# Second layer's expert rows added up in four open PSUM banks instead of scattered and read back; first modulation loads issued ahead of the barrier

## The chip, the cores and the metric

The kernel runs on one core of a Trainium2 chip, as one launch. The metric is the device time of that core in microseconds. The core has a matrix engine (TensorE, PE in the profile, with its weight loads as PEld), a vector engine (DVE), a scalar engine (ACT), GpSimd (POOL) and a sync engine (SP, whose DMA issues stand as SPq), and 16 DMA engines that all of them share. Each engine runs its own instruction stream; the streams meet at semaphores. Matmul results go to PSUM, here eight banks of 128 x 512 float32.

## The reference, cut to what matters

Two layers over 256 context tokens and 256 latent tokens of width 1024, float32. Each layer has a token-mixing half (projection, attention and recurrent heads, output projection) and a channel-mixing half, a mixture of 64 experts with 8 chosen per token. Every half is modulated by vectors that come from `silu(c) @ w_ada`. The second layer returns the latent tokens only.

```python
mod_l = (silu_c @ w_ada[l] + b_ada[l]).reshape(b, 6, 1, D_MODEL)...   # and mod_c from silu(c_ctx)
x_c, x_l = token_mixing(...)
...
# channel mixing; h is (tokens, 1024), 512 tokens in layer 0, 256 in layer 1
scores = sigmoid(h @ router_w); idx = top 8 of the allowed experts; w = scores[idx] / sum * 2.5
def run_block(tok, wt, e):
    xb = h[tok]
    hid = silu(xb @ w_gate[e]) * (xb @ w_up[e])          # 1024 -> 256
    return (hid @ w_down[e]) * wt[:, None]               # 256 -> 1024
y = segment_sum(rows of all experts, token) + shared expert
x_l = x_l + gate_l * rms_norm(y, g_post)
```

## The kernel before

All of it is one Bass program with hand-written semaphores; `build` loops over the two layers (`l`, with `last` for the second), and each engine has one block of code per layer. A first block ahead of an all-engine barrier loads the tokens `X`, the constants and the two condition vectors `HC` (lines 436 to 441), and ACT and DVE prepare small things from them.

**Start of a layer.** SP loads a static list of weight pieces into a ring of three slots: four pieces of `w_ada` (2 MB each, line 508), five of `w_in` (lines 510 to 514), and later ones. Piece n waits until PE has finished with piece n-3. PE first turns the normalised tokens (`transposes`, line 968), then multiplies the four modulation pieces (`ada_piece`, line 978), DVE modulates (line 1433), and the projections follow (lines 1012 and 1015).

**Experts.** The pairs of token and expert are packed into units of 32 rows of one expert; two units (`un` 0 and 1) are a block of 64 slots. Layer 0 runs some 80 blocks, layer 1 runs 48. A row of 1024 is kept as two half rows of 512 on two partitions, so a block fills 128 partitions. SP streams the experts' weights, 3 MB each, through four slots (`load_up` line 533, `load_down` line 538); the gate and up part of a slot is free after the block that used it last has done its up product, the down part after the down product (`reload`, lines 548 and 551). For each block:

- DVE picks the block's table columns and makes a one-hot matrix `OH` (`one_hot`, lines 1749 to 1753); PE multiplies it with token numbers and ranks (`meta`, line 1237, into bank 7); DVE turns the result into a gather index `GIX` and a scatter index `SIXT` (`rows`, lines 1760 to 1765).
- POOL gathers 128 half rows from DRAM `hrows` (line 680) into one of two buffers `XG`. PE turns them (line 1244), ACT moves them to `XGT` (line 913), PE does the gate and up product in 16 matmuls of 32 columns each, four side by side (`up`, line 1254), of which the last four come after the turn of the hidden rows of the block before (line 1313). A float32 matmul is counted as two in the profile, so a block's `up` is x24 and x8.
- ACT and DVE form the hidden rows (lines 919, 923, 1777, 1779). PE does the down product into bank 2 (`down`, line 1279), ACT copies it to one of two `YSB` (line 941), and POOL scatters the 128 half rows to DRAM `yrows` (line 699), at a place for each token and each of its 8 choices. ACT waits on the scatter of two blocks ago before it writes the same `YSB`.

PE's loop is pipelined: iteration b does `up` of block b+1, then the turn of tokens of block b+2, then `down` of block b, then `meta`.

**End of a layer.** When the last scatter has landed, SP reads `yrows` back (line 589, eight loads of 1 MB in layer 1), half of the choices of a token is weighted and added by DVE (line 1820), half by PE with diagonal matrices `DG` (line 1387) that ACT makes from the weights `WK` (DVE, line 1713, one instruction for each tile and choice). DVE adds both to the shared expert's rows in `YS`, then comes the norm (ACT line 952 and 954, DVE lines 1806 to 1811) and the store (line 593).

## Time and profile before

| | us |
|---|---|
| median of 3 runs | 2045.66 |
| lowest, highest | 2041.65, 2048.55 |
| profiled execution, its own time | 2038.08 |
| its span | 2036.3 |
| busy: PE, DVE, ACT, POOL | 1608.0, 898.2, 574.4, 347.3 |
| mean DMA rate | 284 GB/s |

The span is that of one profiled execution. 1.8 us lie around it. The timeline gives, for each group of instructions, its start, its length, the engine, the line, output and input and their shapes, the count, and in brackets how long the engine was idle ahead of it and what ended that. The table of windows gives busy time by engine, the granted clock of PE (1.00 is 2.4 GHz, 0.50 is 1.2 GHz), and the DMA engines' busy share and rate. The stages of the span: layer 0 up to about 1134 us, of which the experts take from about 510 to 1077; layer 1's token mixing to about 1408; layer 1's routing to about 1457; its experts to 1998; its end to 2036.3.

### The profile page before, as it was taken

Reading aid. Unit: us, or ns where it says so; the run is one execution under the profiler, and the core shown is the slowest. Engines: PE = TensorE matmul, PEld = TensorE weight load, DVE = VectorE, ACT = ScalarE, POOL = GpSimd, SP = SyncE. Lnnn points to the kernel's source line nnn. Section 1 sums busy time; section 2 is a strip of 40 time slices with the busy share of each in tenths; the row PEclk is TensorE's granted clock in tenths of the full one; section 3 lists DMA queues with packets and bytes.
Section 4 is the critical chain, followed back from the end, with each engine's and each line's share of the span. In section 5 each row is a group of like instructions: output and inputs, shape, how many; then the busy total and the mean of one; then the engine's idle time right before and its main releaser. Section 6 shows DMA issues by size and latency. Waiting matters only on the chain. (4 is left out here: it accounts for less than half of the span.)

```text
span 2036.3 us, 39515 instructions
## 1 busy us (share of the span) xinstructions
PE 1608.0 (79%) x11503; PEld 697.9 (34%) x11504; DVE 898.2 (44%) x3018; ACT 574.4 (28%) x1197; POOL 347.3 (17%) x357
## 2 busy tenths in 40 slices
PE   3999689868989899888896499867767666766685
PEld 2544554422333333323332365544322222221221
DVE  2154683444444444444455426553533332322334
ACT  2142372222332333323332215143112221211222
POOL 0002300012222222222220001030121111211220
PEclk8999899999999999999998789978888887878998
DMA  8313710467999989998847743624699999999974
GB/s 280 135 70 134 281 64 1 186 234 289 388 405 413 391 348 406 413 358 346 342 156 309 245 152 124 250 105 155 238 410 403 413 401 413 412 405 380 409 308 188
DMA packets 165603, 578.28 MB, mean 284 GB/s; under 512 B 24956, under 2 KB 29792, under 8 KB 148648
## 3 DMA queue, kind: packets, MB, share of 16 engines
q1 hardware_dynamic: 134592, 515.49, 64.7%
q0 software_dynamic: 24256, 60.03, 7.9%
q10 hardware_dynamic: 6696, 1.98, 0.4%
q8 instruction: 37, 0.61, 0.1%
q14 instruction: 22, 0.18, 0.0%
HBM read 557.87 MB, written 37.89 MB: 293 GB/s over the span
## 5 line engine op out<-in xcount | busy, mean ns | idle before, releaser
L1254 PE MATMUL bank<-arena 128*32 128x512 f32 x4160 | 539.1, 638 | 167.4 <-DMA arena<-in_exp_w_up 139.6
L1279 PE MATMUL bank<-arena 128*32 128x512 f32 x2048 | 249.3, 600 | 68.2 <-issue 67.7
L699 POOL DMA_INDIRECT yrows<-arena x128 | 130.1, 1016 | 858.3 <-ACT arena L941 858.3
L1254 PEld LDWEIGHTS bank<-arena 128*32 128x32 f32 x4160 | 125.4, 114 | 355.6 <-issue 327.3
L935 ACT ACTIVATE arena<-bank 128x128 f32<-128x128 f32 x128 | 35.6, 278 | 629.5 <-PE bank L1313 629.5
L1777 DVE TENSOR_TENSOR arena<-arena,bank 64x512 f32<-64x512 f32 x130 | 88.4, 680 | 258.6 <-ACT arena L919 258.6
L680 POOL DMA_INDIRECT arena<-hrows,arena x134 | 137.2, 1024 | 132.5 <-DVE arena L1765 91.9
L1749 DVE COPY arena<-arena 128x12 bf16 (+1 forms) x272 | 60.5, 223 | 188.9 <-issue 188.9
L1012 PE MATMUL bank<-arena 128*128 128x512 f32 (+3 forms) x384 | 132.4, 507 | 11.7 <-DVE arena L1433 11.7
L941 ACT ACTIVATE arena<-bank 128x512 f32<-128x512 f32 x128 | 76.5, 597 | 166.8 <-PE bank L1279 166.8
L1279 PEld LDWEIGHTS bank<-arena 128*32 128x32 f32 x2048 | 60.3, 109 | 163.4 <-issue 161.7
L1244 PEld LDWEIGHTS bank<-arena 128*128 128x128 f32 x528 | 74.0, 209 | 113.3 <-issue 110.8
L1244 PE MATMUL bank<-arena 128*128 128x128 f32 x528 | 98.9, 310 | 2.6 <-issue 1.5
L1012 PEld LDWEIGHTS bank<-arena 128*128 128x128 f32 x384 | 78.0, 214 | 64.4 <-issue 45.8
L1015 PE MATMUL bank<-arena 128*128 128x512 f32 (+1 forms) x256 | 100.0, 552 | 0.0
L919 ACT ACTIVATE arena<-bank 64x512 f32<-64x512 f32 x130 | 77.3, 594 | 40.0 <-PE bank L1254 37.2
L1760 DVE COPY arena<-bank 128x3 f32<-128x3 f32 x134 | 21.8, 163 | 150.2 <-PE bank L1237 149.0
L1175 PE MATMUL bank<-arena 128*128 128x512 f32 x192 | 82.9, 593 | 1.1 <-DVE arena L1613 1.1
L1779 DVE TENSOR_TENSOR arena<-arena 64x256 f32<-64x256 f32 x130 | 54.5, 419 | 65.2 <-ACT arena L923 65.2
L1753 DVE TENSOR_TENSOR arena<-arena 128x512 bf16<-128x512 f32 (+1 forms) x136 | 80.2, 590 | 4.7
L913 ACT ACTIVATE arena<-bank 128x512 f32<-128x512 f32 x132 | 78.8, 597 | 8.0 <-PE bank L1244 3.1
L1313 PEld LDWEIGHTS bank<-arena 64*128 64x128 f32 x256 | 39.6, 201 | 115.9 <-issue 115.9
(305 smaller groups left out, 1856.7 us busy)
## 6 DMA issues: line engine op xcount, KB each, us to landing
arena<-in_exp_w_gate SPq DMA_DIRECT2D x128, 1024.0 KB
arena<-in_exp_w_up SPq DMA_DIRECT2D x128, 1024.0 KB
arena<-in_exp_w_down SPq DMA_DIRECT2D x128, 1024.0 KB
arena<-in_w_ada SPq DMA_DIRECT2D x10, 3072.0 KB, 12.0
arena<-yrows SPq DMA_DIRECT2D x24, 1024.0 KB, 16.3
arena<-in_w_ada SPq DMA_DIRECT2D x8, 2048.0 KB, 12.7
arena<-in_w_in SPq DMA_DIRECT2D x8, 2048.0 KB, 13.4
arena<-in_w_out SPq DMA_DIRECT2D x4, 2048.0 KB, 9.9
```

The source lines that it names most:

```text
L680: pool.indirect_dma_start(out=XG[k], out_offset=None, in_=hrows, in_offset=bass.IndirectOffsetOnAxis(ap=GIX[k], axis=0), bounds_check=2 * ...
L699: pool.indirect_dma_start(out=yrows, out_offset=bass.IndirectOffsetOnAxis(ap=SIXS[u], axis=0), in_=YSB[u], in_offset=None, bounds_check=2 ...
L913: act.activation(XGT, bank[4][:, :].rearrange("p (c u h s) -> p c u h s", c=4, u=2, h=2), ACT.Copy).then_inc(a_xe, 1)
L919: act.activation(HL[0:64, :], bank[0][64:128, :], ACT.Copy).then_inc(a_lo, 1)
L1012: ins = pe.matmul(bank[o % 4][:, c0:width], HT[:, c, tile_of(j)], w[:, c, c0:], start=(c == 0), stop=(c == 7))
L1015: ins = pe.matmul(bank[o % 4][:, c0:], w[:, c, tile_of(j)], HT[:, c, c0:], start=(c == 0), stop=(c == 7))
L1175: ins = pe.matmul(bank[2 * t + hf][:, :], MT[:, c, tile_of(t)], w[:, c, :], start=(c == 0), stop=(c == 7))
L1244: ins = pe.transpose(bank[4][:, c * P:(c + 1) * P], XG[par][:, c:512:4], IDENT)
L1254: ins = pe.matmul(bank[0][r:r + UNIT, :], XGT[:, c, un, hh, :], wv[un][:, :, hh, c, :], start=(c == 0), stop=(c == 3))
L1279: ins = pe.matmul(bank[2][r:r + UNIT, :], HIDT[:, c, UNIT * un:UNIT * un + UNIT], wv[un][:, c, cg * 512:(cg + 1) * 512], start=(c == 0), s ...
L1753: dve.tensor_tensor(OH[:, T0:], IOTA.rearrange("p (u n) -> p u n", u=2).unsqueeze(1).broadcast_to([P, NTS, 2, SLOTS]), RR[:, T0:].unsqueez ...
L1777: dve.tensor_tensor(HL[0:64, :], HL[0:64, :], bank[0][0:64, :], ALU.add).then_inc(v_gu, 1)
```

## The change

**First loads.** Three loads of `w_ada` for layer 0 (6 MB) are issued ahead of the barrier, behind `X` and the constants; the two loads of the condition vectors move to the front. The semaphores of these early loads are new (`sp_first`), so that the ones the ring counts on are not cleared by the barrier. PE does modulation piece 0 ahead of the transposes of the tokens.

**Layout in both layers.** In a block, the half h of a row now lies on partitions 64h to 64h+63 (it was interleaved with the units), so `OH` is half as wide and `meta` writes both halves from the same one-hot. DVE then takes each unit's columns by a mask in two instructions (`picked`), where one copied them.

**Layer 1.** No scatter, no `yrows`, no read-back, no `WK` and no `DG`. The shared expert's down product goes to banks 6, 7, 3 and 1 and stays open there: (6, 7) are the two column halves of token tile 2, (3, 1) of tile 3. `meta` also sums up the slot's weight, split in three bfloat16 parts (`KVW`), and moves to bank 5; PE waits for `v_mc` (DVE has read them) ahead of the third quarter of `up`. DVE keeps token and weight of each slot in `SLOTW` and builds for each block `OHW`, 128 partitions by 2 tiles by 128 tokens: the weight where slot and token meet, else zero. In iteration b PE adds block b-1: four float32 matmuls of 64 rows by 128 columns over 512 (`combine`), just ahead of `down`. There is one `YSB`; ACT writes it when `combine` has read it. POOL no longer scatters, and clears `XG` (128 x 512) ahead of each gather. At the end PE adds the last block, and norm, residual and store work on the banks by halves of 512 columns.

```diff
             def _(sp):
+                sp.dma_start(HC[:, 0, :], ...).then_inc(sp_first[0], 16)
+                sp.dma_start(HC[:, 1, :], ...).then_inc(sp_first[0], 16)
                 for t in range(2):
-                    sp.dma_start(X[:, t, :], ...).then_inc(sp_land[0], 16)
+                    sp.dma_start(X[:, t, :], ...).then_inc(sp_first[2], 16)
...
+                for n in range(3):
+                    sp.dma_start(at(ring[n], 8, 512), w_ada[:, :, n * 512:(n + 1) * 512]).then_inc(sp_land[n], 16)
+                sp.wait_ge(sp_first[2], 64)
-        nc.all_engine_barrier(sems_to_clear=all_sems)
+        nc.all_engine_barrier(sems_to_clear=sems_behind_first)
...
+                if l == 0:
+                    ada_piece(0, 0, 512)
                 transposes(0, (0, 1, 2, 3))
-                for n in range(N_ADA1):
+                for n in range(1 if l == 0 else 0, N_ADA1):
...
                 def shared_down(j):
-                    if j >= 2:
+                    if j >= 2 and not last:
                         pe.wait_ge(a_sd, j - 1)
                     for k in range(2):
-                        ins = pe.matmul(bank[2 + hf][:, :], ..., start=(k == 0), stop=(k == 1))
+                        ins = pe.matmul(bank[acc[j // 2][hf] if last else 2 + hf][:, :], ...,
+                                        start=(k == 0), stop=(k == 1 and not last))
...
+                def combine():
+                    for i in range(2):
+                        for cg in range(2):
+                            r = slice(SLOTS * cg, SLOTS * cg + SLOTS)
+                            ins = pe.matmul(bank[acc[i][cg]][:, :], OHW[r, i, :], YSB[0][r, :], start=False, stop=False)
+                    return ins
...
                         pe.wait_ge(v_hid, b + 1)
+                        if last:
+                            pe.wait_ge(v_mc, b + 4)
                         up(ks, range(2, 3), False)
...
+                    if last:
+                        pe.wait_ge(a_y, b + 2)
+                        pe.wait_ge(v_ow, b + 1)
+                        combine().then_inc(pe_cmb, 1)
                     pe.wait_ge(a_h, b + 1)
                     pe.wait_ge(a_y, b + 2)
...
             # POOL, in the loop
                         pool.sem_inc(pool_go, 1)
+                        if last:
+                            pool.memset(XG[(u + 1) % 2], 0.0).then_inc(pool_z, 1)
+                            pool.wait_ge(pool_z, i * 2 + (u + 2))
                         gather((u + 1) % 2)
+                        if not last: (v_six, a_y, scatter to yrows as before)
...
             # DVE
+                def picked(n, chain):
+                    chain(dve.tensor_scalar(MA[:, 0:NKV], META[:, 0:NKV], COLS[:, 7:8], None, ALU.mult))
+                    dve.scalar_tensor_tensor(out=M3[:, 0:NKV], in0=META[:, NKV:2 * NKV], scalar=COLS[:, 8:9], in1=MA[:, 0:NKV],
+                                             op0=ALU.mult, op1=ALU.add).then_inc(v_mc, 1)
+                def weighted(b, chain):
+                    chain(dve.tensor_copy(S2, SLOTW[:, :, bass.ds(b, 1)].rearrange("p a n -> p (a n)")))
+                    dve.wait_ge(pe_cmb, b + 1)
+                    dve.tensor_scalar(OHW.rearrange(...), IOTA2.rearrange(...), S2[:, 0:1], S2[:, 1:2],
+                                      ALU.is_equal, ALU.mult).then_inc(v_ow, 1)
...
             # DVE, end of layer 1
+                    for i, t in enumerate(TS):
+                        dve.tensor_tensor(SSO[:, t:t + 1], S8[...], S8[...], ALU.add).then_inc(v_so, 1)
+                        dve.wait_ge(a_fs, i + 1)
+                        link(dve.reciprocal(RSTD[:, t:t + 1], SSTD[:, t:t + 1]))
+                        for hf in range(2):
+                            link(dve.scalar_tensor_tensor(out=YS[:, t, c], in0=bank[acc[i][hf]][:, :], ...))
+                            dve.tensor_tensor(X[:, t, c], X[:, t, c], YS[:, t, c], ALU.add).then_inc(v_end, 1)
```

How the change stands in the instruction streams. First PE's loop of layer 1, between the turn of the tokens of block b+2 and the first down product; ISA and TENSOR_LOAD rows are register work. Before:

```order
L1244 MATMUL bank<-arena 128x128 [waits pool_g1]
L1244 MATMUL bank<-arena 128x128 x3
L1361 UNCONDITIONAL_BRANCH
L1363 ISA
L1285 TENSOR_LOAD arena
L1285 ISA x2
L1300 ISA [waits a_y,a_h]
```

And in the changed kernel (its line numbers), up to the branches that choose the weight slot:

```order
L1295 MATMUL bank<-arena 128x128 [waits pool_g1]
L1295 MATMUL bank<-arena 128x128 x3
L1421 UNCONDITIONAL_BRANCH
L1423 ISA
L1336 TENSOR_LOAD arena
L1336 ISA x2
L1366 MATMUL bank<-arena 128x512 [waits v_ow,a_y]
L1366 MATMUL bank<-arena 128x512 x3
L1351 ISA [waits a_y,a_h]
```

Four matmuls come in between the register work and the branches, in every block.

Second, SP at the start of the program, before:

```order
L436 DMA arena<-in_ctx 128x1024
L437 DMA arena<-in_x 128x1024
L438 DMA arena<-in_consts 128x656
L439 DMA arena<-in_consts 128x384
L440 DMA arena<-in_c_ctx 128x8
L441 DMA arena<-in_c 128x8
L432 UNCONDITIONAL_BRANCH [waits sp_land0]
L497 UNCONDITIONAL_BRANCH [waits barrier_Pool_Activation_PE_DVE_SP_release]
L508 DMA arena<-in_w_ada 128x8x512 x3
```

and after, where the three large loads stand ahead of the wait and of the barrier:

```order
L455 DMA arena<-in_consts 128x656
L456 DMA arena<-in_consts 128x384
L459 DMA arena<-in_w_ada 128x8x512 x3
L447 UNCONDITIONAL_BRANCH [waits sp_first2]
L513 UNCONDITIONAL_BRANCH [waits barrier_Pool_Activation_PE_DVE_SP_release]
```

## Rows read from the trace of the kernel before

**Rows 1.** The page's part 2: DMA busy share in 40 slices of 50.9 us.
```profile
DMA  8313710467999989998847743624699999999974
```

**Rows 2.** DMA queues, 1500 to 1950: GB/s in 40 slices; packets, MB, share.
```profile
GB/s 412 414 412 415 412 401 379 412 411 414 412 414 398 407 375 416 412 414 415 411 413 412 413 408 414 412 390 403 413 412 412 375 399 316 391 416 414 411 413 357
...
q1 hardware_dynamic: 36733, 167.75, 92.5%
q0 software_dynamic: 6240, 13.94, 8.0%
```

**Rows 3.** Waits, 1460 to 2000: who for whom, us in total, times, longest.
```profile
PE bank L1254 <- DMA arena<-in_exp_w_up: 137.0, 24, 10.8
...
PE bank L1279 <- issue: 18.4, 28, 1.4
```

**Rows 4.** Windows: length, busy us of PE, PEld, DVE, ACT, POOL, clock, DMA share, GB/s.
```profile
1460.00:1972.00 512.00, 348.10 (x2634) 117.37 (x2626) 162.06 (x677) 114.11 (x228) 90.76 (x89) 0.86 1.00 401
...
1344.70:1346.90 2.20, 2.14 (x6) 0.63 (x6) 0.00 (x0) 1.29 (x2) 2.20 (x5) 0.50 0.06 8
```

**Rows 5.** Timeline of PE: a block after a DMA wait, and one without.
```profile
1558.44 4.58 PE L1254 MATMUL bank<-arena 128*32 128x512 f32 x24 [9.76 <-DMA arena<-in_exp_w_up]
...
1981.15 2.78 PE L1254 MATMUL bank<-arena 128*32 128x512 f32 x24 [0.33 <-issue]
...
1986.79 1.92 PE L1279 MATMUL bank<-arena 128*32 128x512 f32 x16 [0.81 <-issue]
...
1989.18 2.78 PE L1254 MATMUL bank<-arena 128*32 128x512 f32 x24 [0.31 <-issue]
```

**Rows 6.** Timeline of PE: attention scores, two float32 matmuls of 64 rows each.
```profile
1344.76 2.08 PE L1122 MATMUL bank<-arena 64*128 64x512 f32 x4 [0.69 <-ACT arena L859]
...
1357.66 1.13 PE L1122 MATMUL bank<-arena 64*128 64x512 f32 x4
```

**Rows 7.** Timeline of POOL: two memsets of 128 x 512.
```profile
1412.80 1.02 POOL L668 MEMSET arena<- 128x512 f32 x2
```

**Rows 8.** Timeline of DVE in layer 1's routing: first and last of the weights.
```profile
1435.33 0.22 DVE L1713 SCALAR_TENSOR_TENSOR arena<-arena 128x64 f32<-128x64 f32 x1
...
1439.60 0.42 DVE L1699 TENSOR_TENSOR arena<-arena,bank 128x256 f32<-128x256 f32 x1
```

**Rows 9.** Timeline of all engines from the last down product to the end.
```profile
1996.75 0.60 ACT L941 ACTIVATE arena<-bank 128x512 f32<-128x512 f32 x1 [1.54 <-PE bank L1279]
...
1998.21 1.02 POOL L699 DMA_INDIRECT yrows<-arena  x1 [5.53 <-ACT arena L941]
...
2019.21 1.28 ACT L954 ACT_TABLE_LOAD   x1
...
2024.28 1.98 PE L1387 MATMUL bank<-arena 128*128 128x512 f32 x4 [0.52 <-DMA arena<-yrows]
...
2030.72 1.22 DVE L1811 TENSOR_TENSOR arena<-arena 128x1024 f32<-128x1024 f32 x1
```

**Rows 10.** Timeline at token mixing's end: square, scale and add on 512 columns.
```profile
1407.68 0.60 ACT L890 ACTIVATE arena<-bank 128x512 f32<-128x512 f32 x1 [6.18 <-PE bank L1175]
...
1409.12 0.75 DVE L1645 SCALAR_TENSOR_TENSOR arena<-bank,arena 128x512 f32<-128x512 f32 x1
...
1411.29 0.69 DVE L1647 TENSOR_TENSOR arena<-arena 128x512 f32<-128x512 f32 x1
```

**Rows 11.** Timeline of the first 52 us, SP and PE.
```profile
12.17 15.96 SPq L508 DMA_DIRECT2D arena<-in_w_ada  x4
...
19.13 6.55 PE L968 MATMUL bank<-arena 128*128 128x128 f32 x32 [19.13 <-DVE arena L1404]
...
39.67 3.58 PE L978 MATMUL bank<-arena 128*2 128x128 f32 x64 [3.12 <-DMA arena<-in_w_ada]
...
51.09 1.25 PE L1012 MATMUL bank<-arena 128*128 128x264 f32 x2 [5.86 <-DVE arena L1433]
```

**Rows 12.** DMA rate, 0 to 60 us, in 40 slices of 1.5 us.
```profile
GB/s 0 224 366 410 412 333 14 0 0 187 395 382 360 342 351 393 385 397 388 380 374 378 346 359 339 326 308 254 124 244 170 180 195 218 273 368 403 401 351 165
```

More of the change, by code:

```diff
@@ L274, in build @@
         sp_land = [sem(f"sp_land{k}") for k in range(3)]
+        sp_first = [sem(f"sp_first{k}") for k in range(3)]
         sp_up = [sem(f"sp_up{k}") for k in range(NSLOT)]
@@ L404, in build @@
         a_dg = sem("a_dg")
-        v_ys = sem("v_ys")
-        v_fs = sem("v_fs")
+        v_mc = sem("v_mc")
+        v_ow = sem("v_ow")
+        pe_cmb = sem("pe_cmb")
+        pool_z = sem("pool_z")
         v_end = sem("v_end")
@@ L675, in _ @@
                 pool.wait_ge(pool_hr, 16 * NTS)
[L676 to L677 removed]
+                if last:
+                    pool.memset(YSB[0], 0.0).then_inc(pool_clr, 1)
+                    pool.memset(OHW, 0.0).then_inc(pool_clr, 1)
+                else:
+                    for k in range(2):
+                        pool.dma_start(hrows[k:k + 1, :], X[0:1, 0, 0:512]).then_inc(pool_s[k], 16)
                 def gather(k):
@@ L905, in _ @@
                     act.activation(SHS[:, K0:], bank[2 + 2 * k][:, K0:], ACT.Silu).then_inc(a_sh, 1)
-                for j in range(2 * NTS):
+                for j in range(0 if last else 2 * NTS):
                     act.wait_ge(pe_sd, j + 1)
@@ L1661, in _ @@
                 dve.wait_ge(v_pcl, 6)
-                link(dve.tensor_scalar(KV[:, :, :, 0], KV[:, :, :, 0], COLS[:, 0:1], None, ALU.add))
-                for t in range(NT):
-                    link(dve.memset(KV[:, t, :, 1], float(P * t)))
+                link(dve.tensor_scalar(KVX[:, :, :, 0], KVX[:, :, :, 0], COLS[:, 0:1], None, ALU.add))
+                for i in range(2 if last else NT):
+                    link(dve.memset(KVX[:, i, :, 1], float(P * (i + T0 if last else i))))
+                if last:
+                    for i in range(2):
+                        link(dve.tensor_scalar(IOTA2[:, i, :], IOTA, float(P * (T0 + i) + 1), None, ALU.add))
                 dve.wait_ge(pe_rtt, 1)
@@ L1704, in _ @@
                 link(ins)
-                link(dve.tensor_scalar(KV[:, T0:, :, 2], ci, -1.0, float(T), ALU.add, ALU.mult))
+                if not last:
+                    link(dve.tensor_scalar(KV[:, T0:, :, 2], ci, -1.0, float(T), ALU.add, ALU.mult))
                 wsum = WSUM[:, T0:]
@@ L1782, in _ @@
                 pairs = dve.value_load(NPR[0:1, 0:1], min_val=1, max_val=MAXB // 2 + 1)
-                PER = 7
+                PER = 9 if last else 7
+                if last:
+                    dve.wait_ge(pool_clr, 11)
+                    dve.sem_inc(v_ow, 1)
                 with dve.Fori(0, pairs) as i:
```

311 lines of the change are left out of this document (193 added, 118 removed).

## The prediction, made before the changed kernel was run

> **What bounds the kernel now.** I read the slices of the page first: DMA is at 9 tenths or more through the last third and drops only in the last two slices, the end of the kernel [rows 1]. So layer 1's experts live on the weight stream, and what follows them does not. The queue view says how close: from 1500 to 1950 most slices stand at 411 to 416 GB/s, fourteen or so are lower; against 414 they lose some 10 us. Of the traffic 13.94 MB are indirect transfers, which took 8.0% of the 450 us, and weights took 92.5% [rows 2]. The waits confirm it from the other side: PE stood 137.0 us for weights, in 24 waits, the longest 10.8, and 18.4 us for nothing but its own sequencer ahead of the down products [rows 3]. The window 1460 to 1972 is 512 us for 48 blocks at a DMA share of 1.00 [rows 4], 10.7 us each; without PE's waits, 512 - 154 (137 and 17 more that the weight loads waited) = 358 us, or 7.5 us of work each. Two clocks are mixed in that: a block after a long wait starts with x24 in 4.58 us, one without a wait in 2.78, and such a block lasts 1989.18 - 1981.15 = 8.0 us [rows 5].
>
> **Scatter traffic.** Gather and scatter move the same rows, so half of the indirect share goes: 4% of 450 us is 18 us, for 38 of 48 blocks; with the other blocks up to 1972 some 19.5 us. This is the gain of the stream if it stays full.
>
> **combine.** PE gets four float32 matmuls of 64 rows over 512 columns in every block, not in the trace of before. The nearest row is the score product, two such matmuls on opposite row halves and into different banks, as here: 1.13 us at full clock, 2.08 where the window reads a clock of 0.50 [rows 4, 6]. Two matmuls of 128 rows take 1.98 at full clock (L1387 at 2024.28 in [rows 9]), so the halves do run side by side. Four cost 2.0 to 2.3 us at 2.4 GHz. They are issued ahead of the branches that choose the slot, and today PE idles 0.2 to 1.1 us there (0.81 in the block shown [rows 5]); I let 0.6 of that be covered. Net 1.4 us a block. Bounds: 0.9, if all of the gap is covered; 3.5, if the pairs run at 1.2 GHz (2 x 2.08 less 0.6). I take the full clock, because every block shown ends its up product at the full rate even where it began slow. 48 x 1.4 = 67 us of new work against PE's 154 us of slack: PE does not become the bound on average.
>
> **What that does to the stream.** The down part of a slot is given back after `combine`, and in a run of blocks without a wait each block gives its slots back 1.4 us later than now. A wait of PE for weights that lasts 9 or 10 us swallows the lateness; a queue that runs dry inside a run does not. The slices below 411 GB/s show that it runs dry a dozen times already [rows 2], with some two blocks to a run (48 blocks, 24 waits [rows 3]). Lower bound of the new loss: nothing. Upper: 12 x 2 x 1.4 = 34 us. I take the middle, 17 us: stage 19.5 - 17 = 2.5 us shorter. I am least sure of this term. At the end, after the last weights have landed, three blocks run at PE's pace (starts at 1973.97, 1981.15 and 1989.18): + 3 x 1.4 = 4 us.
>
> The Trainium skill (TensorEngine Tiling, Key Properties) speaks against the change: changing the tiling mode drains TensorE, and `combine` puts one more mode between the token turn and the down product. It gives no price. The row pair bounds it: 1.13 us against 1.0 for four quarter-size steps at the steady rate, 0.13 a drain. By the rule, with two drains a block, the term is 1.7 us in place of 1.4 and the total 4 us worse. The sum does not use it.
>
> **DVE, ACT and POOL in a block.** DVE gains one masking step, two small steps for the weight, the copy to `S2` and `OHW` (256 columns), about 1.2 us in all, and loses half of `OH` and the scatter index. Its streams end 6.4 us after `meta` of an 8.0 us block, so it stays inside 9.4. PE's new waits: `v_mc` comes from DVE's second step behind `meta`, while PE has 1.9 us of up product first; `v_ow` comes behind the hidden rows, which PE waits for anyway. Behind a late one stand `combine`, `down` and the slot's release. POOL's clearing is 0.51 us [rows 7] ahead of a gather that no longer stands behind a scatter, and has two blocks of time. All nothing. Layer 0 gets the masking step and the half `OH`: nothing either, since PE sets the pace there at 7.7 us a block and DVE's one-hot is ready 2.4 us ahead of its matmul.
>
> **Routing of layer 1.** The 16 weight instructions go, 1435.33 to 1439.60 [rows 8], but the next step waits for the shared expert's product, which PE ends at 1438.64. So 0.9 us come, and the three added links of the first index chains take them back. Nothing.
>
> **The end.** Now: the last copy ends at 1997.35, the last scatter is issued at 1998.21, then come landing, read-back and sums up to 2026.3, norm and residual up to 2031.94, and the store to 2036.3 [rows 9]. After: copy, one pair of the last `combine` (1.1), two squares on 512 columns (0.6 and 0.2 each: 1.65), add and semaphore 0.4, table load 1.28, root 0.3, reciprocal 0.4, two halves of scale and add 2.86 (1409.12 to 1411.98 [rows 10]); then tile 3, whose root waits for DVE's add behind tile 2: 0.9 and 2.86; then the store, 4.36 as now. The sum with hops is 16.8 us behind 1996.7, against 39.6. Gain 22.8 us.
>
> **The front.** The first `w_ada` load is issued at 12.17 [rows 11]; the DMA engines are idle from 9.0 to 13.5 us, then busy to 46 [rows 12]. With the loads queued behind the constants this gap closes: 4.5 us, less 0.9 for two small issues now ahead of `X`. On top, piece 0 is multiplied before the transposes (19.13 to 25.6), so piece 3 is issued some 11 us earlier and no longer shares the stream with `w_in`; it ends the wait at 39.67 that leads through DVE to the projections at 51.09 [rows 11]. Between 3.6 and 6.6, I take 5 us. From 51.09 PE is busy without a break, so it stays.
>
> **Sum** against the profiled execution: - 5 - 2.5 + 4 - 22.8 = - 26.3 us, 2036.3 to 2010. The median of the runs is 2045.66, 7.6 above the profiled execution's 2038.08; set off from it, 2019.
>
> **Rivals.**
> 1. The stream stays full, as PE's slack of 154 us would have it: then the 17 us don't arise, 2002. For it: waits of 9 us and more swallow six added blocks. Against it: the dry slices.
> 2. PE binds over long stretches: three-block runs become longer than the weights of three experts (3.15 MB at 0.41 MB a us is 7.7 us, a block 9.4), the 34 us arise and the stage is 14.5 us longer than now: 2045.66 - 5 + 14.5 + 4 - 22.8 = 2036.
> 3. Slower than before: `combine` runs at 1.2 GHz, 3.5 us net [rows 6]. Per block 7.5 + 3.5 = 11 us; 48 are 528, and with the 16 us of dry slices now 544 in place of 512: + 32, the last three blocks + 10.5, less 27.8 = + 15, 2060. It decides from about 3.1 us a block. Against it: the half clock shows after waits only [rows 5], and `combine` stands 6 us into a block.
> 4. The early loads don't do what they should: they share the engines with `X` and the constants, the barrier comes later, the front gives nothing. 2024, within the range.
>
> **How the numbers follow.** Forecast 0.50 (2010 to 2027), rival 1 0.22, rival 2 0.16, rival 3 0.04, rival 4 0.08. The range takes in rival 1 and most of rival 2: 2001 to 2035. A measurement here tells 0.3%, 6 us, from no change: same is 2039.5 to 2051.8, to which a strong rival 2 reaches. Faster 0.92, same 0.04, slower 0.04.
>
> **What would show it.** The combine row: x8 in 2.0 to 2.3 us, and a gap ahead of the down product under 0.5. The weight window 3 us or so shorter, with a lower DMA rate than 401 GB/s. PE's wait for weights down from 137 to 60 or 80 us. From the last down product to the end 17 us. The first L1012 (now at 51.09) at 46. Wrong would be: combine groups over 3 us, or a stage whose DMA rate stays at 401 and whose length drops by all 19 us, or waits of PE on `v_ow` or `v_mc`.

## The result, and the profile after

The changed kernel took 1976.65 us (median of 4 runs, 1975.49 to 1985.36), the kernel before beside it 2043.66 (4 runs, 2041.44 to 2048.55): a ratio of 0.968, with a 95% interval of 0.964 to 0.971. That is 67 us less; forecast were 2019 us and a range of 2001 to 2035. The time lies 24 us below the range. Set against each other, the two profiled executions differ by 61.5 us (spans 2036.3 and 1974.8), and they can be cut at four points that both traces show:

| stretch | before, us | after, us | difference | forecast |
|---|---|---|---|---|
| start to the first up product of layer 0 | 436.9 | 429.0 | - 7.9 | - 5 |
| layer 0's experts, to the start of the last down product | 637.6 | 618.1 | - 19.5 | 0 |
| from there to the first up product of layer 1 | 382.5 | 381.8 | - 0.7 | 0 |
| layer 1's experts, to the start of the last down product | 537.8 | 528.3 | - 9.5 | + 1.5 |
| from there to the end | 41.5 | 17.6 | - 23.9 | - 22.8 |

The end and, roughly, the front came as forecast. Two stretches did not: layer 1's experts lost 9.5 us instead of gaining 1.5, and layer 0's experts, of which nothing was expected, lost 19.5. In the changed file L1305 is the up product (L1254 before), L1330 the down product (L1279), L1371 the turning of the hidden rows (L1313), L969 ACT's copy of them (L935), L1366 `combine`.

**Layer 1's experts.** First the window from the first up product to the end of the weight stream, of the changed kernel (columns as in [rows 4]):

```profile
1429.00:1931.00 502.00, 423.72 (x3002) 144.95 (x3003) 191.02 (x822) 113.93 (x228) 70.36 (x92) 0.93 1.00 398
```

and the same window of the kernel before:

```profile
1457.00:1978.00 521.00, 355.47 (x2684) 119.63 (x2684) 166.03 (x697) 114.99 (x230) 93.80 (x92) 0.86 1.00 399
```

PE does 68 us more and the engines of the DMA are full in both (share 1.00, 398 and 399 GB/s). PE's granted clock rose with it, from 0.86 to 0.93. The stream is 19 us shorter at the same rate, which is what was forecast for the scatter's traffic. Of a queue that runs dry behind `combine` nothing is seen. Where PE's new work went is in the waits, 1428 to 1960 (who for whom, us in total, times, longest), against 137.0 us in 24 waits before [rows 3]:

```profile
PE bank L1305 <- DMA arena<-in_exp_w_up: 63.4, 15, 6.8
```

The other part of PE's new work stands behind the stream. The DMA rate in 40 slices of 1.5 us, from 1900 on after, and from 1940 on before:

```profile
GB/s 414 401 410 410 350 421 330 396 396 407 423 426 415 415 410 418 421 418 371 60 49 0 0 0 0 0 0 0 0 0 0 0 0 0 0 0 0 0 0 0
```

```profile
GB/s 418 401 426 399 360 221 178 322 374 223 355 414 421 440 426 393 423 401 429 418 412 372 257 259 60 27 0 0 0 109 0 0 0 0 79 3 0 0 0 0
```

After, the last weight packet starts at 1931.2 and the last down product at 1957.2, 26.0 us later; before, they start at 1978.2 and 1994.8, 16.6 us apart. PE's timeline of the changed kernel in that stretch:

```profile
1940.98 0.23 PE L1288 MATMUL bank<-arena 128*64 128x10 bf16 x4
1941.48 2.78 PE L1305 MATMUL bank<-arena 128*32 128x512 f32 x24 [0.26 <-issue]
1944.19 0.45 PE L1371 MATMUL bank<-arena 64*128 64x64 f32 x2
1944.57 1.06 PE L1305 MATMUL bank<-arena 128*32 128x512 f32 x8
1945.57 0.75 PE L1295 MATMUL bank<-arena 128*128 128x128 f32 x4
1946.24 1.99 PE L1366 MATMUL bank<-arena 64*128 64x512 f32 x8
1948.16 1.92 PE L1330 MATMUL bank<-arena 128*32 128x512 f32 x16
1950.02 0.23 PE L1288 MATMUL bank<-arena 128*64 128x10 bf16 x4
1950.53 2.78 PE L1305 MATMUL bank<-arena 128*32 128x512 f32 x24 [0.28 <-issue]
```

`combine` takes 1.99 us, and neither ahead of it nor behind it is there a gap: the down product starts at 1948.16, before the record of `combine` ends. A block lasts 9.05 us where two blocks before lasted 7.2 and 8.0 [rows 5]: + 1.4 on their mean, as forecast.

**The end.** The timeline of all engines from the last copy on, the rows that answer to [rows 9]:

```profile
1959.20 0.60 ACT L978 ACTIVATE arena<-bank 128x512 f32<-128x512 f32 x1 [2.69 <-PE bank L1330]
1960.09 1.99 PE L1450 MATMUL bank<-arena 64*128 64x512 f32 x8 [0.80 <-ACT arena L978]
1961.26 0.60 ACT L986 ACTIVATE arena<-bank 128x512 f32<-128x512 f32 x1 [1.46 <-PE bank L1450]
...
1962.68 1.28 ACT L989 ACT_TABLE_LOAD   x1
...
1970.18 0.69 DVE L1938 TENSOR_TENSOR arena<-arena 128x512 f32<-128x512 f32 x1
```

Landing, read-back and eight sums are gone; the chain is the one that was written down. From the last down product to the end it is 17.6 us against 41.5.

**The front.** SP's and PE's timeline of the first 44 us (before: [rows 11]):

```profile
4.88 7.74 SPq L459 DMA_DIRECT2D arena<-in_w_ada  x3
19.79 0.54 SPq L526 DMA_DIRECT2D arena<-in_w_ada  x1
```

```profile
16.14 3.59 PE L1026 MATMUL bank<-arena 128*2 128x128 f32 x64 [16.14 <-DMA arena<-in_w_ada]
...
28.02 3.55 PE L1026 MATMUL bank<-arena 128*2 128x128 f32 x121
33.49 2.15 PE L1026 MATMUL bank<-arena 128*2 128x128 f32 x71 [1.93 <-issue]
...
43.45 11.90 PE L1062 MATMUL bank<-arena 128*128 128x264 f32 x40 [5.86 <-DVE arena L1510]
```

Piece 3 is issued when the first product has given back slot 0, at 19.79, and no wait for a DMA stands ahead of its product any more, where before PE waited 3.12 us for it. The projections start at 43.45 in place of 51.09.

**Layer 0's experts.** Here the two traces differ in one row. The kernel before, PE and ACT from one turning of the hidden rows to the down product:

```profile
612.85 1.02 POOL L680 DMA_INDIRECT arena<-hrows,arena  x1 [0.31 <-issue]
...
613.13 0.45 PE L1313 MATMUL bank<-arena 64*128 64x64 f32 x2
...
614.41 0.28 ACT L935 ACTIVATE arena<-bank 128x128 f32<-128x128 f32 x1 [3.75 <-PE bank L1313]
```

```profile
616.18 1.88 PE L1279 MATMUL bank<-arena 128*32 128x512 f32 x13 [0.93 <-issue]
```

The transposes end at 613.58, but ACT's copy of their result starts 0.83 us later, and PE, which waits for the copy ahead of the down product and has its branches to take behind it, stands idle for 0.93. I call this the late copy: one that starts more than 0.1 us behind the transposes. It is there in 76 of the 80 blocks of layer 0, by 0.2 to 1.2 us, 0.92 at the median, and in 26 of the 48 of layer 1. In the changed kernel it is there in 33 of 80 in layer 0 and in none of layer 1; where it is missing, the copy starts 0.04 us behind the transposes:

```profile
601.45 1.02 POOL L705 DMA_INDIRECT arena<-hrows,arena  x1 [0.58 <-issue]
601.46 0.31 PEld L1371 LDWEIGHTS bank<-arena 64*128 64x128 f32 x2 [0.84 <-issue]
601.46 0.45 PE L1371 MATMUL bank<-arena 64*128 64x64 f32 x2
601.94 0.28 ACT L969 ACTIVATE arena<-bank 128x128 f32<-128x128 f32 x1 [2.95 <-PE bank L1371]
```

PE's waits ahead of the down product, over layer 0, in the kernel before (437 to 1076.4) and the changed one (429 to 1047):

```profile
PE bank L1279 <- issue: 49.3, 76, 1.8
```

```profile
PE bank L1330 <- issue: 28.9, 40, 1.8
```

### The profile page after: what moved, and what is told of

It reads as the page before. It is cut to its first block and busy times, and to the rows that moved or that the text cites. A ratio compares the mean times of both kernels' runs of the same rounds, so it can differ in the third digit from the quotient of the medians.

```text
span 1974.8 us, 40623 instructions
## 1 busy us (share of the span) xinstructions
PE 1671.9 (85%) x11863; PEld 721.0 (37%) x11864; DVE 911.4 (46%) x3217; ACT 569.5 (29%) x1189; POOL 322.7 (16%) x358
## 5 line engine op out<-in xcount | busy, mean ns | idle before, releaser
L1305 PE MATMUL bank<-arena 128*32 128x512 f32 x4160 | 529.4, 628 | 100.8 <-DMA arena<-in_exp_w_up 69.1
L1330 PE MATMUL bank<-arena 128*32 128x512 f32 x2048 | 249.2, 601 | 30.4 <-issue 29.7
L1305 PEld LDWEIGHTS bank<-arena 128*32 128x32 f32 x4160 | 123.2, 113 | 283.6 <-issue 265.8
L969 ACT ACTIVATE arena<-bank 128x128 f32<-128x128 f32 x128 | 35.5, 277 | 496.1 <-PE bank L1371 483.9
L732 POOL DMA_INDIRECT yrows<-arena x80 | 81.1, 1013 | 408.8 <-ACT arena L978 408.8
L1836 DVE COPY arena<-arena 128x12 bf16 (+1 forms) x272 | 54.4, 200 | 188.1 <-issue 188.1
L1330 PEld LDWEIGHTS bank<-arena 128*32 128x32 f32 x2048 | 57.1, 109 | 155.1 <-issue 151.8
L1847 DVE TENSOR_SCALAR arena<-bank,arena 128x3 f32<-128x3 f32 (+1 forms) x134 | 29.8, 222 | 155.5 <-PE bank L1288 154.4
L1366 PE MATMUL bank<-arena 64*128 64x512 f32 x384 | 95.4, 615 | 0.0
L724 POOL MEMSET arena<- 128x512 f32 x48 | 25.2, 525 | 408.7 <-DVE arena L1865 408.7
```

Source lines behind the costliest of these rows:

```text
L732: pool.indirect_dma_start(out=yrows, out_offset=bass.IndirectOffsetOnAxis(ap=SIXS[u], axis=0), in_=YSB[u], in_offset=None, bounds_check=2 ...
L1305: ins = pe.matmul(bank[0][r:r + UNIT, :], XGT[:, c, hh, un, :], wv[un][:, :, hh, c, :], start=(c == 0), stop=(c == 3))
L1330: ins = pe.matmul(bank[2][r:r + UNIT, :], HIDT[:, c, UNIT * un:UNIT * un + UNIT], wv[un][:, c, cg * 512:(cg + 1) * 512], start=(c == 0), s ...
L1366: ins = pe.matmul(bank[acc[i][cg]][:, :], OHW[r, i, :], YSB[0][r, :], start=False, stop=False)
```

## The experiments

They ran in five sets; the kernels of a set share a chip and the runs of the kernel before. Those runs were the first finding: the kernel before took 2022.3, 2020.7, 2041.8, 2021.9 and 2020.0 us in the five, while it had taken 2043.7 in the shown pair. Ratios are to the kernel before in the same set.

### What made layer 0 faster: first set (before 2022.3)

Nearly all late copies of the shown traces have the gather 1.32 us behind the scatter's start; in the blocks of the changed kernel where it stood at 1.58, the copy was on time. So theory A was that the late copy comes from this distance, and that the change had moved it by the longer index chain. Two kernels put one small POOL step ahead of the gather, `e1_before_pool_step` on the kernel before and `e2_after_pool_step` on layer 0 of the changed one:

```diff
+pool.memset(SPACE, 0.0).then_inc(pool_nm, 1)
+pool.wait_ge(pool_nm, i * 2 + (u + 1))
+pool.sem_inc(pool_go, 1)
 gather((u + 1) % 2)
```

> The kernel before with one small POOL clearing (256 columns, some 0.3 us) and its wait ahead of each gather of the block loops, both layers. Theory A (timing of the gather): in the blocks of layer 0 that don't wait for weights, ACT's copy of the hidden rows (L935 before) starts 0.8 to 1.2 us behind the end of the two transposes, and always about 1.55 us behind the start of the gather, when the gather is issued 0.3 us behind the scatter's end; with 0.6 us or more between them, as in every second block of the changed kernel, it starts 0.04 us behind. Then the copy starts at once in all blocks, the gap ahead of the down product goes, a block takes 7.0 to 7.3 us in place of 7.88, and layer 0 is 35 to 60 us shorter. Theory B (the narrower one-hot or the new row layout made layer 0 faster): nothing here changes, 2044 us, or up to 0.3 us more a block.

> The changed kernel with the same POOL clearing and wait ahead of each gather of layer 0 alone. Theory A: the late copy goes in the other half of layer 0's blocks too (it is there in 40 of 80), 25 to 40 us less than the changed kernel, about 1945 us; the down-to-down period of layer 0 falls from 7.63 to 7.1 or 7.2. Theory B: as the changed kernel, 1977 us, or a little more.

Two others lengthen DVE's chain on the kernel before by the same two steps, ahead of the indices or behind them:

```diff
+chain(dve.tensor_copy(TK[:, 3:4], TK[:, 1:2]))
+chain(dve.tensor_copy(TK[:, 3:4], TK[:, 1:2]))
```

> The kernel before with two more one-column DVE copies in a chain ahead of the two indices of a block, so that the gather's index comes 0.4 to 0.5 us later. Nothing else changes; POOL has no new instruction. Theory A: the gather now starts 0.6 to 0.7 us behind the scatter's end in place of 0.3, the copy of the hidden rows starts at once, layer 0 is 35 to 60 us shorter. Theory B, and the theory that DVE's chain sets the pace: no gain, or up to 0.5 us a block more, 40 us longer.

> The kernel before with the same two DVE copies, but behind the indices and ahead of the one-hot. Theory A: the gather is issued as before, 0.3 us behind the scatter, so the late copy stays and layer 0 takes what it took, within 3 us. The rival of theory A that any longer DVE chain does it (fewer collisions of DVE with PE or POOL): as the run with the later index.

Measured: 2026.7 (ratio 1.002, 1.001 to 1.003), 1978.5 (0.979), 2024.3 (1.001, 0.999 to 1.002) and 2023.4 (1.000, 0.999 to 1.002). None of the four has one late copy in layer 0, not even e4, whose gather stands at 1.32 us in 75 of 78 places. Theory A as I had it is gone: a gather at 1.32 us is not enough for a late copy. The totals of e1, e3 and e4 lie outside every reading that I had written down, because the kernel before was 21 us faster in this set without any step; e2 came out near the 1977 of theory B, which says nothing for B, since the late copies were missing without a step as well.

### Is it the program or the execution: second set (before 2020.7)

> The kernel before, unchanged, profiled once more. In the three runs above that were built on it the kernel before took 2022 us where it had taken 2044, and none of them shows the late copy of the hidden rows, not even the one whose gather is issued 0.3 us behind the scatter in 75 of 78 places; so theory A as stated (the distance of the gather) has fallen. Theory C: the late copy belongs to the execution (the chip that it ran on), not to the program. Then this run, where it takes about 2022 us, has the copy 0.04 us behind the transposes in all blocks, a layer 0 of 617 to 622 us in place of 637.6, and a layer 1 of 535 to 542. Theory D: it belongs to the program and two more DVE steps or a POOL step are enough to end it; then the late copy is there in 76 of 80 blocks, whatever the total.

> The changed kernel, unchanged, on the same chip as the kernel before. Theory C: layer 0 takes the same as in the kernel before on this chip, within 3 us, and the change is worth 45 to 49 us here in place of 67 (7.6 at the front, 24 at the end, the rest in layer 1's experts). Theory D: 60 us or more, 20 of them in layer 0.

The kernel before, unchanged: 2023.0 us, no late copy, 613.7 us for layer 0 where the shown execution took 637.6. Its rows at the same place, the gather 1.32 us behind the scatter as ever:

```profile
611.23 1.01 POOL L699 DMA_INDIRECT yrows<-arena  x1 [8.33 <-ACT arena L941]
612.55 1.02 POOL L680 DMA_INDIRECT arena<-hrows,arena  x1 [0.31 <-issue]
...
612.84 0.45 PE L1313 MATMUL bank<-arena 64*128 64x64 f32 x2
613.33 0.28 ACT L935 ACTIVATE arena<-bank 128x128 f32<-128x128 f32 x1 [2.96 <-PE bank L1313]
```

and its waits ahead of the down product, over layer 0:

```profile
PE bank L1279 <- issue: 14.2, 30, 1.8
```

The changed kernel: 1976.2 us (ratio 0.978, 0.975 to 0.980), no late copy, 620.3 us for layer 0. So theory C holds in this: whether there are late copies at all comes with the execution and not with the program. The change is worth 44.5 us where it is absent (I had written 45 to 49) and 67 where it is present. Layer 0 then does not get shorter: 613.7 to 622.1 us over eight executions of the kernel before and its variants, 615.2 to 620.3 over six of the changed one and its variants. Beside c1, c2 is 6.6 us longer there, more than the 3 that I had allowed and inside this scatter. With late copies four executions of the changed kernel and its variants took 618.1 to 624.9 us. Its waits give a part of them back: without late copies PE waits 14.1 us for weights in layer 0, with 33 of them 5.6.

### The front (same set, and third set)

`e5_after_front_undone` issues the three loads behind the barrier and multiplies piece 0 behind the transposes; `e10_first_product_late` (third set, before 2041.8) puts back the product alone:

```diff
-if l == 0:
-    ada_piece(0, 0, 512)
 transposes(0, (0, 1, 2, 3))
-for n in range(1 if l == 0 else 0, N_ADA1):
+for n in range(N_ADA1):
```

> The changed kernel with the first three modulation loads issued behind the barrier and the first modulation product behind the transposes, as before. Prediction: 5 us longer than the changed kernel (3.6 to 6.6); by the changed kernel's trace, in which the first projection came 7.6 us earlier, 7 to 8 us. Rival: the early loads are worth nothing by themselves and the 7.6 us come from the order of the first inputs, which stays: under 2 us. Layer 0 and layer 1 take as long as in the changed kernel, within 2 us.

> The changed kernel with its early loads, but with the first modulation product behind the transposes, as before. With loads and product both put back the kernel took 7.4 us more. Prediction: the gap of 3.6 us belongs to the loads, the rest to the product ahead of the transposes, which lets piece 3 be issued earlier: so 1.5 to 4 us more than the changed kernel. Rival: everything comes from the loads, which are issued 7.3 us earlier (4.88 in place of 12.17): under 1 us.

Measured: e5 1983.6 against 1976.2, 7.4 us more; the projections start at 52.06, in c2 at 44.45. e10: 1987.8 us, and they start at 52.19, while two other variants of the changed kernel in its set (e7 and e9, below) have them at 45.23. Both readings of e10 missed, since it gives up 7.0 us where I had 1.5 to 4, or under 1: early loads without the early product give nothing at all. Its rows, of SP and PE:

```profile
4.58 8.16 SPq L459 DMA_DIRECT2D arena<-in_w_ada  x3
30.59 0.54 SPq L526 DMA_DIRECT2D arena<-in_w_ada  x1
```

```profile
28.60 5.42 PE L1026 MATMUL bank<-arena 128*2 128x128 f32 x192
40.78 3.60 PE L1026 MATMUL bank<-arena 128*2 128x128 f32 x64 [6.76 <-DMA arena<-in_w_ada]
```

Three pieces lie ready in three slots, but the fourth needs the first slot, and that comes free with the first product. It is issued at 30.59, and PE waits 6.76 us for it. In the kernel before it was issued at 27.59, in the changed one at 19.79: these 7.8 us are about the gain at the projections. What the early product gives without the early loads was not run.

### What combine costs (second and third set)

`e6_combine_8_columns` cuts `combine` in the loop to 8 of 512 columns, which leaves most of the routed sum out; `e7_combine_twice` issues it twice, which adds the routed rows twice. The edit of e6:

```diff
-ins = pe.matmul(bank[acc[i][cg]][:, :], OHW[r, i, :], YSB[0][r, :], start=False, stop=False)
+ins = pe.matmul(bank[acc[i][cg]][:, 0:8], OHW[r, i, :], YSB[0][r, 0:8], start=False, stop=False)
```

> The changed kernel with each of combine's four matmuls in a block cut to 8 of its 512 columns, which leaves most of the routed sum out of the output. What combine costs the stream. Prediction (the slots come back 1.4 us later and the queue runs dry behind them, 17 us in all, + 4 us in the last three blocks): layer 1's experts end 15 to 21 us earlier than in the changed kernel. Rival (the stream stays full, PE's waits swallow combine, as the trace with a DMA rate of 401 GB/s suggests): 3 to 6 us earlier, the last three blocks alone, while PE's waits for weights grow by 70 to 90 us.

> The changed kernel with combine's four matmuls issued twice in each block of the loop, so that the routed rows are added twice. With combine once, the weight transfers of layer 1's experts take 501 to 503 us from first to last and the last down product starts 26 us behind their end; with 8 columns of it 503.6 and 16.5. Theory E (PE's waits for weights, 63 us, are the only buffer; as long as some are left the stream does not feel PE): 48 x 2.0 = 96 us of new work against 63 us of waits, so the buffer is used up; layer 1's experts get 30 to 40 us longer and the waits go to under 10 us. The prediction's dry queue (each added microsecond per block costs the stream a third of itself at once): 17 us for 1.4 a block gives 24 us more for 2.0, and the waits are not used up (30 us or more are left).

| kernel | combine, us a block | first up product to end of weights | PE's waits for weights | granted clock | end of weights to last down product |
|---|---|---|---|---|---|
| e6, 8 columns | 0.6 | 501.4 | 111.4 | 0.87 | 16.5 |
| c2, changed kernel | 2.0 | 500.4 | 62.7 | 0.94 | 25.6 |
| shown, changed kernel | 2.0 | 502.3 | 63.4 | 0.93 | 26.0 |
| e7, twice | 3.9 | 503.1 | 12.4 | 0.98 | 36.7 |

e6 does not take `combine` away, but cuts it to a third; its row is

```profile
1936.95 0.62 PE L1366 MATMUL bank<-arena 64*128 64x8 f32 x8
```

e6 took 1966.7 us against 1976.2, e7 1996.7 in a set with late copies, in which the changed kernel was not run. The 9.5 us of e6 lie between my two readings, 15 to 21 and 3 to 6, and its waits grew by 49 us in place of 70 to 90. The waits of PE in e7, from 1435 to 1976:

```profile
PE bank L1305 <- issue: 14.6, 22, 7.7
PE bank L1305 <- DMA arena<-in_exp_w_up: 12.4, 6, 3.4
```

`combine` costs the stream nothing, not even twice: its length stays within 3 us. The waits pay the larger part, 49 us for the 1.4 us a block between e6 and c2 and 50 for the 1.9 between c2 and e7. They don't pay all: 46 blocks times 1.9 is 87 us. The clock gives another part. The 1472 records of the up product in the window, c2 and e7 (length, busy PE and PEld, clock, DMA share, GB/s):

```profile
1431.90:1932.30 500.40, 202.39 (x1472) 49.52 (x1472) 0.94 1.00 399
1434.40:1937.50 503.10, 183.99 (x1472) 45.34 (x1472) 0.98 0.99 397
```

With fewer and shorter waits PE stood longer at the full clock, and the same work took 18 us less. The rest of `combine`'s price lies behind the stream: 9 us from e6 to c2, 11 from c2 to e7. The prediction's dry queue has fallen. My own expectation for e7, that the experts get 30 to 40 us longer, was off too: they took 539.9 us, where the changed kernel took 526.0 (c2) and 528.3 (shown). I had set 96 us of work against 63 us of waits and left out what the clock gives back; 12 us of waits were still left.

### The scatter's traffic (third set, before 2041.8)

`e8_before_no_scatter_rows` leaves the kernel before as it is, but layer 1's scatter drops every row, so that the routed part of layer 1 is missing from the output:

```diff
-bounds_check=2 * (TOPK * T + 1) - 1, oob_is_err=False
+bounds_check=1 if last else 2 * (TOPK * T + 1) - 1, oob_is_err=False
```

> The kernel before with the bound of layer 1's scatter set so low that it drops every row: POOL still issues it, no row is written, and the routed part of layer 1 is missing from the output. The price of the traffic alone. Prediction: half of the indirect share, 19.5 us less in layer 1's weight stream (524.7 from first to last in the kernel before on such a chip, so 505), the end of the kernel as before: 2001 us where before takes 2021. Rival: the scatter's price lies in more than its bytes (its packets of 2 KB hold the engines up, or its place ahead of the gather): 25 us or more; or less than 10, if the weights' own packets set the rate.

Measured: 2021.1 us, 20.7 less than the kernel before (ratio 0.990, 0.987 to 0.992). The set has late copies (76 of 80 blocks in layer 0), so the total that I wrote down, 2001 from 2021, is met as a difference. From the first up product to the end of the weights it takes 502.5 us where the shown execution of the kernel before took 521.2: by this pair the traffic's price is 18.7 us, and the changed kernel's stream is as long (502.3). The kernel before and its variants without late copies have a longer stream, 523.5 to 527.1 us in eight executions, and in the second set the difference from c1 to c2 is 23.1 us. Why their stream is 2 to 6 us longer than that of the shown execution stays open; so the price is 19 to 23 us, by the set. In layer 1, where no row is written any more, e8 still has 32 late copies in 48 blocks: the data that the scatter writes is not what makes them.

### A faster version (third and fourth set)

What is left behind the stream is PE's own pace. In `e9_combine_bf16` the operands of `combine` are bfloat16, so that the profile counts each matmul once and no longer twice. The operands are rounded, the sum stays in float32:

```diff
-OHW = at(o - 512, 2, P)
+OHW = at16(o - 512, 2, P)
+YSW = at16(o - 1024, 512)
...
-ins = pe.matmul(bank[acc[i][cg]][:, :], OHW[r, i, :], YSB[0][r, :], start=False, stop=False)
+ins = pe.matmul(bank[acc[i][cg]][:, :], OHW[r, i, :], YSW[r, :], start=False, stop=False)
```

> The changed kernel with the expert rows and the weighted one-hot of layer 1 held as bfloat16, so that combine's four matmuls go through TensorE in one pass in place of four; the products are summed in float32 as before, the operands are rounded. Combine should take 0.5 to 0.8 us in place of 2.0. Behind the end of the weight stream this gives back most of the 9.5 us that combine costs there: 6 to 8 us less than the changed kernel, 1968 to 1970. If the dry queue counted, 12 us or more.

> The changed kernel with bfloat16 operands in combine, beside k4 on the same chip. In its first run it took 1971.2 and layer 1's experts 517.0 us in place of 528.3, with PE 16.6 us behind the end of the weight stream in place of 26.0. Expected 6 to 10 us less than k4.

> The changed kernel, unchanged, as the measure of k3, and of the change on this chip: 1976 us on each chip so far, whether the kernel before takes 2021 or 2042. On a chip with the late copy it should have 33 to 35 late copies in layer 0, on another none, and a layer 0 of 616 to 622 us on both.

In the fourth set (before 2021.9) k3 took 1965.8 us (1964.3 to 1967.4) and k4, the changed kernel, 1977.8 (1976.2 to 1980.1): 11.9 us less, a little more than the 6 to 10 that I had written, and less than both kernels of this case. e9, the same kernel, took 1971.2 beside 2041.8, just over the 1968 to 1970 expected. The timeline of k3's last blocks:

```profile
1940.54 0.61 PE L1367 MATMUL bank<-arena 64*128 64x512 bf16 x4
1941.08 1.92 PE L1331 MATMUL bank<-arena 128*32 128x512 f32 x16
...
1948.17 0.61 PE L1367 MATMUL bank<-arena 64*128 64x512 bf16 x4
```

`combine` takes 0.61 us, as with 8 columns in e6, a block 7.6, and from the end of the weights to the last down product it is 18 us in place of 26 (16.6 in e9). PE waits 110.5 us for weights again. The profiled executions of k3 and k4 differ by 10.6 us; 9.0 of them lie in layer 1's experts (519.2 against 528.2) and 0.8 in the end.

### The late copy once more (fourth and fifth set)

The kernels of e3 and e4 were run again in the hope of a set that has it.

> The kernel before with two more one-column DVE copies ahead of the two indices, once more; on a chip where the kernel before takes 2040 us or more, and so has the late copy. Theory F (the late copy needs the gather to be issued within 1.4 us of the scatter): the gather stands at 1.63 us, no block has a late copy, layer 0 takes 617 to 622 us in place of 637.6, and the kernel 2024. Theory G (the chip alone decides): 76 of 80 blocks late, 637 us or more. On a chip without the late copy (before at 2021) it says nothing new: 2024.

> The kernel before with the same two copies behind the indices and ahead of the one-hot, on the same chip. Theory F: the gather stays at 1.32 us, 75 of 80 blocks are late, layer 0 takes 637 us or a little more. If DVE's own work at the time of the transposes decides it, not POOL's: as k1, or between the two. On a chip without the late copy: 2022.

> The kernel before with two more DVE copies ahead of the indices, in another set. If the kernel before takes 2040 us in this set: theory F (gather within 1.4 us of the scatter) says no late copy and 2024; theory G (the set alone) says 76 late of 80 and 2040 or more. If it takes 2021, the late copy is not in this set and the run says only that.

> The same two copies behind the indices. In a set with the late copy, theory F: 75 of 80 late, 2042. If DVE's work decides: as m1.

The sets took 2021.9 and 2020.0 with the kernel before, and none of the four has a late copy (2023.6, 2021.6, 2023.8 and 2019.9 us). The fourth set ran on the same chip, number 0, as the third, in which every kernel had them. So the number of the chip does not decide it either. These runs say nothing for or against the gather's distance.

## Why the prediction was wrong, by its own steps

**Where the miss lies.** The profiled pair differs by 61.5 us where 26.3 were forecast. Of the 35.2 us between them 19.5 lie in layer 0, 11.0 in layer 1's experts, 2.9 in the front, 1.1 in the end and 0.7 between the layers' experts. The step of the prediction that failed is the dry queue, 17 us. Layer 0's share is not the change's: without late copies the gain is 44.5 us, which 2045.66 - 2001 = 44.7 would just have taken in.

**What bounds the kernel: right.** Layer 1's experts are bound by the stream in both kernels, 399 and 398 GB/s at a share of 1.00.

**Scatter traffic, 19.5 us: right in kind.** 18.9 in the shown pair, 18.7 in e8, 23.1 from c1 to c2. The working was loose: 18 us for 38 scatters are 21 for the 45 that lie ahead of the end of the weights, not 19.5.

**combine, 2.0 to 2.3 us: right,** 1.99. **Net 1.4 a block: right by luck.** The gap that I let cover 0.6 us was no sequencer gap but the wait for the late copy; one of the two blocks before that the comparison uses has it. In c1, without late copies, two blocks at the end take 7.2 and 7.3 us:

```profile
1954.25 2.78 PE L1254 MATMUL bank<-arena 128*32 128x512 f32 x24 [1.25 <-DMA arena<-in_exp_w_up]
...
1961.44 2.78 PE L1254 MATMUL bank<-arena 128*32 128x512 f32 x24 [0.34 <-issue]
...
1968.76 2.78 PE L1254 MATMUL bank<-arena 128*32 128x512 f32 x24 [0.32 <-issue]
```

Against these the 9.05 us are 1.8 more, nearly all of `combine`. In layer 1 of the changed kernel there was no late copy in any execution.

The Trainium skill (TensorEngine Tiling, Key Properties) says that a change of the tiling mode drains TensorE. In the rows above the down product starts 1.92 us behind `combine`'s start, ahead of the end of its record, so no cost of its own shows: the 1.8 us that a block became longer are less than those 1.92.

**The dry queue, 17 us: this step failed.** I counted a slice below 411 GB/s as a queue that had run dry and multiplied it by the lateness of a slot. But such slices are there without `combine` as well, and from e6 to e7, 0.6 to 3.9 us a block, the stream moves by less than 3 us. The slack is PE's 137 us of waits, and beside them what the clock gives back when they shrink; even in e7, with 12.4 us of waits left, nothing reached the stream. I had this as rival 1 (2002 us, chance 0.22) and gave it too little; the sentence on what would be wrong named it: a stage whose rate stays and whose length drops by all 19 us. Its 43 us of gain are near the 44.5 measured without late copies, in part by luck: traffic, front and end gave some 7 us more than forecast, and the last blocks cost 6 more.

**The last blocks, 4 us: too small by 5 to 6.** When the weights end, PE is further behind: 26.0 us or 2.9 blocks of 9.05 are left, where before it was 16.6 us or about two. To the longer block comes about one more block: 9.4 us, and e6 gives 9.1 of it back. The window shows it too: up to the last weights 46 up products are done in the changed kernel (1472 records of 32 each), 47 in e6 and in the kernel before (1504). That PE is further behind because it runs closer to the stream's pace is my reading; e7, with 36.7 us left, goes the same way. Without late copies the term is 10.3 us (15.3 in c1, 25.6 in c2).

**The end, 22.8 us: right,** 23.9, by the links that were written.

**The front, 5 us: too small.** 7.6 us in the shown pair and 7.4 in e5, above the upper bound of 6.6. I took the gap of the DMA engines as the price and piece 3 as an extra. e10 shows the reverse: the pieces that come early wait in their slots, and the term is how much earlier the first product frees slot 0, which is 7.8 us and not the 11 that I had for it.

**Layer 0, nothing: right of the change, wrong for the shown pair.** Without late copies both kernels take the same there, within what executions scatter. In the shown pair 19.5 us stand there, and the one difference found is that the kernel before had 76 late copies and the changed one 33. The profile had shown it: I read the idle 0.3 to 1.1 us ahead of nearly every down product as the sequencer's, without asking when the copy had started that it waits for. Why the changed kernel has fewer is not settled. In both sets that had late copies, the kernels built on the changed one had 33 to 35 of 80 and those built on the one before 76. In the first the gather stands at 1.58 us in about half of the blocks, and of 136 late copies in four executions one fell on such a block; in the latter it stands at 1.32 throughout. A set with late copies in which this distance is moved alone was not met.

**The sum.** The terms, corrected by the second set, which has no late copies: - 7.6 for the front, - 23.1 for the stream, + 10.3 behind it, - 23.9 for the end, together - 44.3; measured 44.5. The rest of the 67 us comes and goes with the late copy.

## What to carry to other kernels

A stage that lives on a stream does not feel new work on an engine that waits for the stream, as long as waits are left; here the rising clock stretched this room further. Price the work where the stream has ended, times the blocks that are then still open, and allow for one block more. A load that is issued early is worth nothing by itself in a ring of slots: ask which product frees the slot that the late piece needs. And before an idle gap is booked to the sequencer, look at when the operation started that the engine waits for, and run the kernel before again on another occasion, since a gap of 0.3 us in each of 80 blocks can belong to the execution.

## What the runs showed of the hardware

- In some sets of runs and not in others, with the same program, ACT starts 0.2 to 1.2 us late (0.92 at the median) on the result of two small transposes, in 76 of 80 blocks, while it starts at once (0.14 us) on the result of the matmuls issued behind them. The kernel before takes some 21 us more in such sets (2041.8 and 2043.7 against 2020.0 to 2022.3). Copies were late almost only in blocks that PE had reached without a wait for weights, and while POOL issued a gather 1.3 to 1.4 us behind a scatter's start; the late ones start some 1.5 us behind the gather's start. It does not need the scatter to write rows (32 of 48 blocks in layer 1 of e8). What it is stays open.
- Float32 matmuls of 64 rows by 512 columns, four of them on alternating row halves, take 1.99 us; in bfloat16 0.61 us. In float32 over 8 columns they take 0.62 us, as long as the bfloat16 ones over 512.
- More work on PE between waits raised its mean granted clock (0.87, 0.94 and 0.98 in e6, c2 and e7), and the same 1472 records took 202.4 us at 0.94 and 184.0 at 0.98.
- Dropping every row of a scatter by its bound takes its traffic away (indirect transfers 16.33 MB before, 8.25 in e8; the stream 18.7 us of 521 shorter) and leaves POOL's 1.0 us for issuing it.
